# The last down products by token tile and column half, and the value projection ahead of the key projection

## The reference, cut to what matters

```python
ff = conv_ffn(h, ffn_w_in[layer], ffn_conv_w[layer], ffn_conv_b[layer], ffn_w_out[layer])   # ... @ w_out: (256 x 2816) @ (2816 x 1024)
h = layer_norm_2(ALPHA_2 * h + ff, ln_ffn_g[layer], ln_ffn_b[layer])
if layer == N_A_LAYERS - 1:
    k_flat, v_flat = jnp.split(h @ shared_w_kv, 2, axis=-1)      # keys 256 columns, values 256 columns
...
q = (h @ w_q)                                                   # 1024 columns
```

## Time and profile before

| what | value |
|---|---|
| median of 3 runs | 1553.13 us (1552.24 to 1554.76) |
| time of the profiled execution | 1553.6 us |
| its span | 1551.8 us |
| PE, DVE, ACT busy | 1376.5, 693.0, 514.5 us |
| mean granted TensorE clock | 0.942 |
| PE share of the chain that ended last | 72% |

### The profile page before, as it was taken

The page is one execution under the profiler, slowest core; times in us unless marked ns, Lnnn a source line. Parts: engine busy times, 40 slices in busy tenths (PEclk is TensorE's granted clock), DMA queues, the critical chain, the costliest instruction groups (busy, mean ns, idle before and its releaser), DMA issues.

```text
span 1551.8 us, 19682 instructions
## 1 busy us (share of the span) xinstructions
PE 1376.5 (89%) x7728; PEld 972.1 (63%) x7728; DVE 693.0 (45%) x1319; ACT 514.5 (33%) x949; POOL 120.8 (8%) x135
## 2 busy tenths in 40 slices
PE   6987799988699887999986989789999796899997
PEld 3854544343357545444333988559998694499985
DVE  0253502121303534112115479568776626477765
ACT  1343211111112512111102423316765426166653
POOL 1012000000000211000001036030000003000000
PEclk9989799999989796999997999899999898999999
DMA  9430379999945104999999533954575530346650
GB/s 326 167 136 28 136 329 421 421 421 422 381 163 203 69 1 186 423 421 422 420 422 328 190 105 112 133 198 162 162 257 205 165 136 1 112 155 193 216 190 27
DMA packets 128050, 347.72 MB, mean 224 GB/s; under 512 B 8209, under 2 KB 84263, under 8 KB 103397
## 3 DMA queue, kind: packets, MB, share of 16 engines
q1 hardware_dynamic: 122576, 330.19, 56.4%
q0 software_dynamic: 4528, 15.84, 4.3%
q10 hardware_dynamic: 868, 0.63, 0.1%
HBM read 342.44 MB, written 4.19 MB: 223 GB/s over the span
## 4 chain that ended last, share of the span: by engine, by line
PE 72%; DMA 14%; DVE 9%; ACT 3%; issue 2%; SPq 0%; DVEq 0%; POOL 0%; ACTq 0%
PE bank L1549 17%; DMA slot<-in_w_up 13%; PE bank L1740 9%; PE bank L1880 7%; PE bank L1881 7%; PE bank L1882 7%; PE bank L1750 4%; PE bank L2001 2%; PE bank L2003 2%; PE bank L2005 2%; PE bank L1915 2%; PE bank L1761 2%; ACT arena L795 1%; DVE res L1095 1%; DVE x_tok L1098 1%
## 5 line engine op out<-in xcount | busy, mean ns | idle before, releaser
L1880 PE MATMUL bank<-x_high,w_high 128*128 128x256 f32 x912 | 261.7, 287 | 2.3 <-DVE x_low L1347 2.3
L1881 PE MATMUL bank<-x_low,w_high 128*128 128x256 f32 x912 | 260.8, 286 | 0.0
L1882 PE MATMUL bank<-x_high,w_low 128*128 128x256 f32 x912 | 260.5, 286 | 0.0
L1740 PE MATMUL bank<-slot,arena 128*64 128x512 f32 x1024 | 227.5, 594 | 29.3 <-DMA slot<-in_w_up 16.5
L756 ACT ACTIVATE w_high<-slot 128x1024 fp32r<-128x1024 f32 x174 | 174.3, 1051 | 178.8 <-PE bank L1882 94.5
L1740 PEld LDWEIGHTS bank<-slot,arena 128*64 128x64 f32 x1024 | 77.9, 137 | 175.5 <-issue 175.5
L1880 PEld LDWEIGHTS bank<-x_high,w_high 128*128 128x128 f32 x912 | 178.0, 195 | 4.4 <-issue 4.3
L1881 PEld LDWEIGHTS bank<-x_low,w_high 128*128 128x128 f32 x912 | 178.1, 195 | 0.0
L1882 PEld LDWEIGHTS bank<-x_high,w_low 128*128 128x128 f32 x912 | 177.9, 195 | 0.0
L756 ACT ACTIVATE arena<-bank 128x512 f32<-128x512 f32 (+6 forms) x156 | 77.9, 517 | 253.6 <-PE bank L1797 95.5
L1549 PE MATMUL bank<-slot,arena 128*128 128x512 f32 (+1 forms) x320 | 136.6, 586 | 4.2 <-ACT arena L756 3.3
(11 more groups left out here) (273 smaller groups left out, 1963.6 us busy)
## 6 DMA issues: line engine op xcount, KB each, us to landing
slot<-in_w_gate SPq DMA_DIRECT2D x64, 1024.0 KB, 19.3
slot<-in_w_up SPq DMA_DIRECT2D x64, 1024.0 KB, 20.8
slot<-in_w_down SPq DMA_DIRECT2D x64, 1024.0 KB, 21.3
slot<-in_ffn_w_in SPq DMA_DIRECT2D x44, 1024.0 KB, 7.5
slot<-in_ffn_w_out SPq DMA_DIRECT2D x22, 1024.0 KB, 5.0
slot<-in_hgrn_w_in SPq DMA_DIRECT2D x16, 1024.0 KB, 6.5
slot<-in_w_in SPq DMA_DIRECT2D x10, 1024.0 KB, 11.4
slot<-in_w_o SPq DMA_DIRECT2D x8, 1024.0 KB, 7.0
```

Source lines behind the costliest of these rows:

```text
L1740: last = mm(banks_gu["gu".index(m)][rows, :], xe[:, 4 * half + c, rows], ws[e][:, c, :], start=(half == 0 and c == 0), stop=(half == 1 and ...
L1880: mm(dst, high[:, k, :], x_high[:, k, :], start=(k == 0), stop=False)
L1881: mm(dst, high[:, k, :], x_low[:, k, :], start=False, stop=False)
L1882: last = mm(dst, low[:, k, :], x_high[:, k, :], start=False, stop=(k == KD - 1))
```

## The change

Three edits.

1. TensorE's tile-wise end of both down projections is cut once more, by column half: tile 0 half 0, tile 0 half 1, tile 1 half 0, tile 1 half 1, each with all remaining units (one in layer 2, two in layer 3).
2. ScalarE's and VectorE's split of the key weights `kv0` moves from in front of the layer norm to behind it; the wait for `down_done` goes.
3. The values `vv` are multiplied before the keys `kv0`, and ScalarE copies the values before it turns to the keys. The bank order of the plan follows.

```diff
@@ plan
-    for n in ("kv0", "vv", "kR0", "kR1", "kR2", "kR3"):
+    for n in ("vv", "kv0", "kR0", "kR1", "kR2", "kR3"):
@@ ScalarE
-            act.wait_ge(sem("down_done"), DOWN - 1)
-            split_slot(3, names[0], KV_UNIT)
             norm_std(5)
             transposed_split(2, "z", whole=True)
+            split_slot(3, names[0], KV_UNIT)
             split_slot(3, names[1], KV_UNIT + 1)
+            b = produced(act, (3, "vv"))
+            drained(copy(G["v"], b[:, :].rearrange("p (c n) -> p c n", c=2)), (3, "vv"))
             b = produced(act, (3, "kv0"))
             split_slot(3, names[2], KV_UNIT + 2)
             drained(copy(G["kraw"], b[:, :].rearrange("p (c n) -> p c n", c=2)), (3, "kv0"))
-            b = produced(act, (3, "vv"))
-            drained(copy(G["v"], b[:, :].rearrange("p (c n) -> p c n", c=2)), (3, "vv"))
@@ VectorE
-            low_slot(3, names[0], KV_UNIT)
             norm(5, 2, "z", True)
...
-            for n in range(1, 5):
+            for n in range(5):
                 low_slot(3, names[n], KV_UNIT + n)
@@ TensorE, feed_forward
-                def unit(i, tiles):
+                def unit(i, tiles, halves=range(2)):
...
-                            for h in range(2):
+                            for h in halves:
                                 mm(...)          # three times: high*high, high*low, low*high
...
                 for t in range(NT):
-                    for i in range(by_tile, DOWN):
-                        last = unit(i, [t])
-                        if i < DOWN - 1 and t == NT - 1:
-                            last.then_inc(sem("down_done"), 1)
+                    for h in range(2):
+                        for i in range(by_tile, DOWN):
+                            last = unit(i, [t], [h])
+                            if i < DOWN - 1 and t == NT - 1 and h == 1:
+                                last.then_inc(sem("down_done"), 1)
@@ TensorE, after layer 2
             next_x(2, "z", 5)
-            pair(3, "kv0", KV_UNIT)
             u = loaded(pe, (3, "kv1"))
             b = reuse(pe, (3, "vv"))
             ...                                  # vv
             done(last, (3, "vv"))
+            pair(3, "kv0", KV_UNIT)
             evacuated(pe, (3, "kv0"))
```

## The result

| kernel | median, us | ratio to the kernel before on the same chip, 95% interval |
|---|---|---|
| before | 1552.68 (1551.14 to 1554.82, 8 runs) | |
| after | 1558.05 (1555.27 to 1559.93, 8 runs) | 1.0032 [1.0021, 1.0043] |

The change makes the kernel slower by 5.0 us by the ratio (5.4 by the medians). The profiled execution after took 1558.63 us with a span of 1556.8 us, 5.0 more than the span before. The forecast was +3.8 us: the right sign and the right places, with two prices of the clock too low in the profiled execution: one on the values, put at nothing, and one at layer 3's end.

The account below looks back on a forecast made before the run. TensorE was taken to bound the kernel, with 72% of the chain of waits. The terms -1.99 + 2.75 + 1.4 + 0.25 + 1.4 made +3.8 us: 1557.0 us against the median, 1557.4 for the profiled execution; range 1553.6 to 1560.0.

Parts of the forecast that it names:

- Part 1: Layer 2's end: the layer norm and the dense work behind it start 1.99 us earlier.
- Part 2: Behind layer 2's norm: the moved split of kv0 is hidden by the value product of 7.07 us, costing 0.
- Part 3: Before the spreading products: TensorE newly waits for ScalarE's split of sq1 and copy of the keys, +2.75 us.
- The sentence on the low stretch of the seam: Seam: the existing low-clock stretch falls on the values instead of the keys, at about the same price, within 0.15 us.
- Part 4: Behind the new wait after the keys: one low-clock stretch costs +1.4 us, ends 0 and 3.0.
- Part 5: Layer 3's end: the wait for g_low grows to 2.9 us and the norm gets its second half 0.25 us later.
- Part 6: Behind the grown wait at layer 3's end: a low-clock stretch costs +1.4 us, ends 0 and 2.0.
- (b): Rival: only one of the two gaps loses the clock, 1555.5 us, or none, 1554.1 us; chance 0.28.
- (c): Rival: the seam keeps its clock and the change is not slower, 1551.8 us without low stretches in new gaps; chance 0.10.
- (d): Rival: weight loads cost where halves are apart, 1560.2 us with half of 36 more before the norms' second halves; chance 0.05.

Follow-up runs that it names:

- e6: Kernel after with matmuls nobody reads in its two new gaps, 20 behind the keys and 11 at layer 3's end; 1558.58 us, ratio 1.0028.
- e1: Kernel before with the first edit alone, both down-product ends by tile and half; 1553.72 us, ratio 1.0001.
- e5: Kernel after with the query product sq0 put between the keys and their spreading; 1554.71 us, ratio 1.0008.
- e4: Kernel after with ScalarE copying the keys to kraw before splitting sq1; 1555.01 us, ratio 1.0009.
- e3: Kernel after with halves in layer 2 only, layer 3's end by tile as before; 1557.01 us, ratio 1.0024.
- e8: e7 with matmuls nobody reads in TensorE's three idle pieces during the norm between the layers; 1547.41 us, ratio 0.9966, the fastest of the study.
- e9: Kernel before with matmuls nobody reads in TensorE's three idle pieces during the norm between the layers; 1551.43 us, ratio 0.9983.
- e2: Kernel after with the first edit undone in both layers; values before keys and the moved split stay; 1556.02 us, ratio 1.0014.
- e7: e5 with only the last unit cut by half at both down-product ends; 1551.48 us, ratio 0.9991.

## Why the prediction was right, step by step

- **Part 1, the earlier norm (-1.99):** measured -1.97 for tile 1's first addition and for the start of the dense work.
- **Part 2, the moved split (0):** right; TensorE goes from the values to the keys without a wait.
- **Part 3, the wait behind the keys (+2.75):** the last key matmul starts at 1251.92 and the keys' pace is 0.12 us, so TensorE could have gone on at 1252.04; the spreading starts at 1254.78, +2.74. The recorded idle time is 2.58.
- **The sentence on the low stretch of the seam (within 0.15 us):** wrong, the first mis-sized term. Values and keys together took 14.24 us before (1240.11 to 1254.35) and 15.29 after (1236.75 to 1252.04): +1.05. I let the low stretch move along with the work. It did not: the clock rose between 22.6 and 23.0 us after the last unit's start before (1243.2 to 1243.6) and between 22.6 and 22.8 after (1241.9 to 1242.0). The dense work began 1.97 us sooner, and those 1.97 us ran at half speed.
- **Part 4, the clock behind the keys (+1.4):** from spreading to heads the profile went from 25.35 to 26.84 us, +1.49; e6 gives 1.47.
- **Part 5, order at layer 3's end (+0.25):** e1 shows it alone, +0.26.
- **Part 6, the clock at the end (+1.4, upper end 2.0):** the second mis-sized term. +2.77 in the profile after (66.27 - 63.25 - 0.25), 0 in e1, 1.5 in e5, 2.8 in e4. The low stretch was 6.8 us in the profile after, twice the one whose price I took. The upper end was worked out wrongly: all 18 matmuls at half speed take twice their 4.1 us and lose about 4, not 2.0; 14 of them fell into the low stretch, and 2.8 us were lost. Over the runs e3 against after puts the end at 1.2 us in all, with an interval that reaches beyond 3. So 1.4 may have been about right as a mean, which is not shown; as this execution's price it was half the size.
- **Rivals:** (b) is what e1 alone does at the end. (c) fell: 0.50 was granted in all of 1236.7 to 1241.9. It had the second idle piece, between the tiles' transposes, at 3.8 us; it was 4.6, since the first tile's transposes now ran ahead of the clock's fall, in 1.1 us and not 1.97. (d) fell: layer 2's last unit takes 5.21 us from first to last start in e1 and e3 as before, and layer 3's end is 0.26 us longer in e1. The Trainium skill (TensorE: Matmul & The Clock Gate, the part on how LDWEIGHTS gets the stationary operand into the array) says that one load can serve many matmuls. These traces show none that does: 7728 loads beside 7728 matmuls before and after; cutting the halves apart cost 0.26 us at most, which the order explains.

The two mis-sized terms (+1.05 and +1.37) make 2.4 of the 2.6 us between the 3.8 forecast and the 6.4 of the trace; the rest is in parts 1, 3 and 4 and the middle, none above 0.1. Of the 6.4 us 1.39 were hidden in the span by an earlier start of the seam. That the time of the profiled execution, 1558.63, lies only 1.2 us above the forecast 1557.4 is luck to that extent.

The earlier start goes with the clock of the stages ahead and not with an edit. Ahead of layer 2's last down unit 0.50 was granted for 140 us in the profile before and 123 after. In all twelve profiles the unit starts later where that time is longer: at 1218.55 to 1219.30 us with 120 to 123 us, at 1220.00 to 1220.17 with 137, at 1220.64 to 1222.17 with 140. e4, which has the change's edits, is in the last group (1221.44). Why that time differs from one execution to the next is not known.

## What to carry to other kernels

When a product is moved in front of another to cover a chain, look at what it used to cover behind: here the values had hidden ScalarE's split and copy for the keys, and another product without that need (e5) has to take the place. When accumulation is cut finer to release a consumer sooner, cut only what lies behind the last wait; units in front of it are work that fills the wait. And an idle chain between two dense stages is paid twice, in its length and in the half-speed start behind it; matmuls that nobody reads, put only into time that is idle anyway, gave 2.6 us on the kernel before (1.9 of them at the seam in the profile) and about 4 of the 5.3 us of the best. It is no sure gain: in e6 they saved 4.2 us in the two gaps of the profile and the kernel was not faster.

## What the hardware showed that I had not expected

- The same wait of 2.8 us for `g_low` was followed by a granted clock of 1.00 (e1) and by 6.8 us at 0.50 (kernel after). The length of a wait alone did not decide.
- Starting dense work 1.97 us earlier after an idle seam did not bring the clock's rise earlier. In all ten profiles without fillers in the seam the clock was low from 9.0 to 22.7 us after the first matmul of the last down unit, with the dense work starting at 17.5, 18.6 or 19.5. With the seam filled (e8, e9) it was not low there at all.
- The heads, busy in part only, took 200.0 (e9), 200.6 (e2), 201.3 to 201.6 (most) or 205.4 us (e6) to layer 3's down products with an unchanged list of instructions from the heads to those products; in e6 they had 13.5 us at 0.50 in one piece. Most of these times go with the low stretches in them, 13.7 us in e9, 17.1 in e2, 20.5 in the kernels before and after, 27.3 in e6, but not all: e5 and e7 have 17.1 us and took 201.36.
